# A kernel of two transformer blocks: the output projection's PSUM banks in another order, and VectorE's last gated rows ahead of a feed

## What is computed

```python
mod = jax.nn.silu(c) @ w_ada + b_ada
sh1, sc1, gt1, sh2, sc2, gt2 = jnp.split(mod, 6, axis=-1)
h = adaln(rms_norm(x, g_mix), sh1, sc1)
proj = h @ w_in
...
y_a = swa_attention(q_a, k_a, v_a, sinks) @ w_o_swa
y_b = moba_attention(q_b, k_b, v_b) @ w_o_moba
mixed = jax.nn.sigmoid(gate_a) * y_a + jax.nn.sigmoid(gate_b) * y_b
x = x + gt1[:, None, :] * (mixed @ w_out)
h = adaln(rms_norm(x, g_mlp), sh2, sc2)
u = jnp.square(jax.nn.relu(h @ w_up))
x = x + gt2[:, None, :] * (u @ w_down)
```

## Time and profile before

| | us |
|---|---|
| median of three runs | 1648.8 |
| the three runs | 1648.47, 1648.8, 1655.24 |
| span of the profiled execution | 1650.3 |
| TensorE matmuls busy | 1508.9 (91%) |
| TensorE weight loads busy | 1280.3 (78%) |
| VectorE busy | 1239.3 (75%) |
| ScalarE busy | 867.1 (53%) |
| GpSimd busy | 226.0 (14%) |

### The profile page before, as it was taken

The page is one execution under the profiler, slowest core; times in us unless marked ns, Lnnn a source line. Parts: engine busy times, 40 slices in busy tenths (PEclk is TensorE's granted clock), DMA queues, the critical chain, the costliest instruction groups (busy, mean ns, idle before and its releaser), DMA issues.

```text
span 1650.3 us, 24315 instructions
## 1 busy us (share of the span) xinstructions
PE 1508.9 (91%) x9872; PEld 1280.3 (78%) x9872; DVE 1239.3 (75%) x1845; ACT 867.1 (53%) x1194; POOL 226.0 (14%) x203
## 2 busy tenths in 40 slices
PE   2999989999999998999999899999879779799986
PEld 2889888999998977899998477767568547577764
DVE  4868898888877865899986578877468783688862
ACT  2537536445444642544545467766434474477752
POOL 5050010000005000000002310034111202210121
PEclk7899999999999999999999999999969999999998
DMA  9854497999964448588880499999657421799973
GB/s 321 279 171 138 153 327 269 324 316 319 307 200 135 148 141 297 183 283 294 282 293 26 179 357 422 423 375 400 250 193 252 157 102 54 268 402 422 420 281 140
DMA packets 191871, 425.00 MB, mean 258 GB/s; under 512 B 8344, under 2 KB 136784, under 8 KB 175504
## 3 DMA queue, kind: packets, MB, share of 16 engines
q1 hardware_dynamic: 170688, 334.53, 56.8%
q0 software_dynamic: 13824, 63.62, 10.3%
q10 hardware_dynamic: 7248, 25.30, 3.8%
HBM read 397.20 MB, written 26.21 MB: 257 GB/s over the span
## 4 chain that ended last, share of the span: by engine, by line
PE 66%; DVE 15%; DMA 9%; ACT 6%; issue 3%; POOL 1%; SPq 0%; POOLq 0%; ACTq 0%; DVEq 0%
PE psum L700 62%; DVE acc L1956 4%; DVE w_lo L1933 3%; DMA h_row<-h_rows,token_at 3%; PE psum L1163 2%; DMA raw<-in_w_ada 1%; DMA dn_raw<-in_moe_wd 1%; DVE gu_lo L1968 1%; ACT att_room L1866 1%; ACT w_hi L1431 1%; DVE steps_room L2028 1%; DVE tmp L1989 1%; DMA both<-y_rows,row_at 1%; ACT gu_hi L1445 1%; DVE x L2440 1%
## 5 line engine op out<-in xcount | busy, mean ns | idle before, releaser
L1933 DVE TENSOR_TENSOR w_lo<-raw,w_hi 128x1024 fp32r<-128x1024 f32 x250 | 304.5, 1260 | 75.7 <-ACT w_hi L1431 75.5
L700 PE MATMUL psum<-h_lo,w_hi 128*128 128x256 f32 (+1 forms) x1280 | 341.3, 290 | 0.0
L700 PE MATMUL psum<-h_hi,w_lo 128*128 128x256 f32 (+1 forms) x1280 | 341.1, 289 | 0.2 <-DVE w_lo L1933 0.2
L1431 ACT ACTIVATE w_hi<-raw 128x2048 fp32r<-128x2048 f32 x125 | 238.7, 1911 | 101.4 <-DMA raw<-in_w_up 50.4
L700 PE MATMUL psum<-h_hi,w_hi 128*128 128x256 f32 (+1 forms) x1280 | 264.2, 299 | 9.3 <-DVE tmp L2170 5.7
L1956 DVE SCALAR_TENSOR_TENSOR acc<-raw,cond,acc 128x1024 f32<-128x1024 f32 x196 | 258.3, 1325 | 11.4 <-DMA raw<-in_w_ada 6.8
L700 PEld LDWEIGHTS psum<-h_lo,w_hi 128*128 128x128 f32 x1280 | 250.8, 196 | 1.5
L700 PEld LDWEIGHTS psum<-h_hi,w_lo 128*128 128x128 f32 x1280 | 250.5, 196 | 1.8 <-DVE w_lo L1933 0.5
L700 PEld LDWEIGHTS psum<-h_hi,w_hi 128*128 128x128 f32 x1280 | 200.0, 197 | 32.1 <-issue 17.4
L1968 DVE TENSOR_TENSOR gu_lo<-raw,gu_hi 128x1024 fp32r<-128x1024 f32 x160 | 188.5, 1221 | 28.1 <-ACT gu_hi L1445 28.1
L1445 ACT ACTIVATE gu_hi<-raw 128x2048 fp32r<-128x2048 f32 x84 | 159.9, 1905 | 0.0
(11 more groups left out here) (264 smaller groups left out, 2687.5 us busy)
## 6 DMA issues: line engine op xcount, KB each, us to landing
raw<-in_w_ada SPq DMA_DIRECT2D x48, 1024.0 KB, 6.9
raw<-in_w_mod SPq DMA_DIRECT2D x48, 1024.0 KB, 5.7
raw<-in_w_in SPq DMA_DIRECT2D x34, 1024.0 KB, 5.4
raw<-in_w_up SPq DMA_DIRECT2D x32, 1024.0 KB, 6.0
raw<-in_w_down SPq DMA_DIRECT2D x32, 1024.0 KB, 5.9
raw<-in_moe_wg SPq DMA_DIRECT2D x32, 1024.0 KB, 11.3
raw<-in_moe_wu SPq DMA_DIRECT2D x32, 1024.0 KB, 10.3
dn_raw<-in_moe_wd SPq DMA_DIRECT2D x32, 1024.0 KB, 9.8
```

The lines of the kernel that those rows point to most:

```text
L700: return e.matmul(o, lhs, rhs, start=start, stop=stop, skip_group_check=True)
L1431: e.activation(flat_unit(w_hi[:, split_slot(u)]), raw[:, slot, :], ACT.Copy).then_inc(*w_rounded.on(u))
L1933: e.tensor_tensor(flat_unit(w_lo[:, split_slot(u), k]), raw[:, slot, part], plain(flat_unit(w_hi[:, split_slot(u), k])), ALU.subtract).the ...
```

## The change

1. The output units write banks 2, 3, 0, 1 in place of 0, 1, 2, 3; TensorE and VectorE both follow.
2. On VectorE the low parts of rows 0 and 1 stay where they were. feed(g0+20), which stood at j = 3 behind the sum of row 2, is taken out of there, and so is the low part of row 2. At j = 4, behind the outputs and sum of row 3, now stand the low parts of rows 2 and 3, then feed(g0+20) with its weight unit ahead of its modulation piece, then feed(g0+21).

ScalarE, SyncE and GpSimd keep their orders.

```diff
--- before.py
+++ after.py
@@ -536,6 +536,7 @@
             return head_rstd[:, first + tile // 2 * 2, at_:at_ + 3:2]
 
         GATE_BANKS = (0, 7)
+        OUT_BANKS = (2, 3, 0, 1)
         POOL_BANKS = (0, 1, 2, 3), (4, 6, 7, 0)
 
         paired = {table.batches.index([(row, item[2]) for _, row in conditions(item[1], item[2])]): p
@@ -1016,7 +1017,7 @@
                     close(g)
                 stage = ("m", l)
                 for j in range(4):
-                    b = j
+                    b = OUT_BANKS[j]
                     product(g0 + 21 + j, b, S, h_hi1, h_lo1, lambda i: e.wait_ge(*rounded.at("mix", l, i // 2)),
                             lambda i: e.wait_ge(*rest.at("mix", l, i // 2)))
                     freed[b] = [(added, ("out", l, 2 * j + 1))]
@@ -2160,6 +2161,13 @@
                             normalise(l, h)
                     if k >= 3:
                         pair_lo(l, k - 3)
+                def mix_low(q):
+                    ya = tbuf(2 * (q % 2)).rearrange("p (m n) -> p m n", n=S)
+                    c = slice(2 * q, 2 * q + 2)
+                    e.wait_ge(*rounded.at("mix", l, q))
+                    e.scalar_tensor_tensor(out=h_lo1[:, c, :], in0=ya, scalar=0.5, in1=plain(h_hi1[:, c, :]),
+                                           op0=ALU.mult, op1=ALU.subtract).then_inc(*rest.on("mix", l, q))
+
                 for j in range(9):
                     if 1 <= j <= 4:
                         q = j - 1
@@ -2177,15 +2185,17 @@
                         q = j - 5
                         e.wait_ge(*multiplied.at(g0 + 21 + q))
                         for m in range(2):
-                            add_x(psum[:, q, m * S:(m + 1) * S], l, 2, 2 * q + m, 0).then_inc(
+                            add_x(psum[:, OUT_BANKS[q], m * S:(m + 1) * S], l, 2, 2 * q + m, 0).then_inc(
                                 *added.on("out", l, 2 * q + m))
-                    if j < 8:
+                    if j == 4:
+                        mix_low(2)
+                        mix_low(3)
+                        late = table.feeds[g0 + 20]
+                        feed(g0 + 20, [f for f in late if f[1][0] == "w"] + [f for f in late if f[1][0] != "w"])
+                    if j < 8 and j != 3:
                         feed(g0 + 17 + j)
-                    if 1 <= j <= 4:
-                        e.wait_ge(*rounded.at("mix", l, q))
-                        c = slice(2 * q, 2 * q + 2)
-                        e.scalar_tensor_tensor(out=h_lo1[:, c, :], in0=ya, scalar=0.5, in1=plain(h_hi1[:, c, :]),
-                                               op0=ALU.mult, op1=ALU.subtract).then_inc(*rest.on("mix", l, q))
+                    if 1 <= j <= 2:
+                        mix_low(q)
                 columns(g0 + 24)
                 norm_scale(("m", l))
                 modulate(("m", l))
```

## The result

| kernel | median, us | runs | ratio to before, 95% interval |
|---|---|---|---|
| before | 1650.68 | 20 | 1 |
| the change | 1654.58 | 20 | 1.0024 [1.0013, 1.0035] |
| before, beside the repeat | 1649.85 | 35 | 1 |
| the change, repeated | 1657.47 | 12 | 1.0036 [1.0020, 1.0051] |

The change costs 3.9 us (2.1 to 5.8). Repeated with the last experiments it cost 5.9 us (3.3 to 8.4), and both together, weighted by their intervals, give 1.0028, 4.6 us (3 to 6). It is slower, by less than the 0.5% that the prediction called no change.

A forecast was written before the change was run, and what follows sets the result against it. It took VectorE to bound layer 0 and late columns to hold TensorE in layer 1. 6.05 + 0.35 = 6.4 us on the profiled 1650.3 gave 1656.7, less 1.5 for the median: 1655.2 us, 8-in-10 range 1648.5 to 1659.5.

The forecast's parts named there:

- Layer 1, the columns: Layer 1, ahead of unit 78: columns start 3.55 us later, TensorE's wait grows from 1.96 to 5.5 us.
- Layer 1, the clock: Layer 1, modulation product and unit 78: lowered clock behind the longer wait costs 2.5 us, ends 0 and 3.1.
- What is behind it goes along: Layer 1, behind unit 78: addition, modulation and load all slip with its end, 6.05 us later.
- Rival C: Layer 1: the clock doesn't fall, so +3.55 + 0.35, 1652.7 us; chance 12%.
- Layer 0: +0.35 us: Layer 0: TensorE's won time is given back behind unit 21, net +0.35 us, ends -1.7 and +2.
- the new wait ahead of the squares' sum: Layer 0, behind unit 22: TensorE waits 3.2 us for VectorE's addition.
- Rival A: Layer 0: TensorE's wait sets the stage, -7.7 us there, layer 1 still loses 6.05: 1647 us; chance 7%.
- Rival B: Layer 0: three bunched loads bring unit 24 later than about 235, +2 us; 1657.4 or over; chance 20%.
- Rival D: Both layers: the change reaches layer 1 only in form and does nothing in layer 0; 1655.5 us; chance 3%.
- the lower case of A: Both layers: layer 0's wait is won and layer 1's columns are not held up either; 1641 us; chance 3%.

The follow-up runs named there:

- layer 0 alone: The change with its new VectorE order in layer 0 only, new banks in both layers, against the kernel before: 1649.64 us, 1.0002.
- banks alone: The new bank order with VectorE's order as before, against the kernel before: 1650.58 us, 1.0000.
- piece early: New banks; layer 0's moved modulation piece stays ahead of outputs 3, layer 1 in old order; against the kernel before: 1649.30 us, 0.9991; again 1649.74 us, 0.9989.
- layer 1 alone: The change with its new VectorE order in layer 1 only, new banks in both layers, against the kernel before: 1655.04 us, 1.0030.
- order alone: VectorE's new order in both layers with the old banks 0 to 3, against the kernel before: 1653.29 us, 1.0018.
- five idle matmuls: The change plus five unused matmuls in TensorE's layer 1 wait for the columns; against the kernel before: 1653.32 us, 1.0026; again 1652.19 us, 1.0010.
- ten idle matmuls: The change plus ten unused matmuls of 512 columns ahead of layer 1's modulation product; against the kernel before: 1660.81 us, 1.0069.
- columns still earlier: The piece early kernel with layer 1's columns also moved ahead of the sum of row 3: 1649.74 us, 1.0000 against the kernel before.
- columns-first kernel: The change with the columns of batch 8 written directly behind the sum of row 3, ahead of the low parts: 1650.54 us, 1.0003 against the kernel before.

## Why the prediction was right, and where not

Distances in layer 1 in us, one profile each. "Norm" is the norm's reciprocal; at full clock x56 takes 7.00 and x60 7.45. The first five rows have the old order, the next four the new one. Unit 77's end is the start of the matmuls that follow it (629.24 before), x56 are the matmuls behind the wait for the columns, x60 those behind the load.

| kernel | unit 77 to modulation product | x56 | x60 | both | unit 77 to the norm |
|---|---|---|---|---|---|
| before | 2.91 | 7.00 | 10.47 | 17.47 | 42.92 |
| layer 0 alone | 2.90 | 7.00 | 8.96 | 15.96 | 41.06 |
| banks alone | 2.91 | 8.56 | 8.96 | 17.52 | 42.96 |
| piece early | 2.90 | 8.52 | 8.94 | 17.46 | 42.80 |
| piece early, again | 2.91 | 7.00 | 10.47 | 17.47 | 43.02 |
| **change** | 6.47 | 9.17 | 8.94 | 18.11 | 47.14 |
| change, again | 6.48 | 8.70 | 8.94 | 17.64 | 46.54 |
| layer 1 alone | 6.48 | 8.57 | 8.95 | 17.52 | 46.35 |
| order alone | 6.48 | 9.30 | 7.46 | 16.76 | 45.59 |
| five idle matmuls | 6.48 | 7.00 | 7.45 | 14.45 | 43.49 |
| five, again | 6.48 | 7.00 | 10.47 | 17.47 | 46.56 |
| ten idle matmuls | 9.57 | 6.98 | 10.46 | 17.44 | 49.45 |
| columns still earlier | 2.18 | 8.51 | 7.45 | 15.96 | 40.49 |

**Layer 1, the columns: +3.55 us. Right.** 3.57 us in four profiles, the wait 5.53 for 5.5. That they bound the stage is shown by the columns-first kernel, which takes them back alone and loses the loss.

**Layer 1, the clock: +2.5 us. This step failed.** Behind the wait itself the clock did fall each time: 9.17, 8.70, 8.57 and 9.30 us, 1.6 to 2.3 over full clock, on average 8.94 where the five profiles with the old order have 7.62. But the prediction compared x56 with a kernel before that happened to be at full clock there, and left x60 at its 10.47, the slow value: "What is behind it goes along". In fact the low clock falls behind the first wait, the second, or both, and costs 1.5 to 3.7 us over the two in these nine profiles. Together the two stretches take 17.2 us on average in the old order and 17.5 in the new one: 0.3 us, not 2.5. From the scatter of the nine, that difference is known to about 1 us, so 2.5 is excluded and 1 is not. With 3.57 that is 3.9 us, and the norm comes 3.85 us later on average (46.41 for 42.55), where 6.05 was forecast. The load behind unit 78, put at 5.37 us as the shortest seen, took 5.04 to 5.47 us, which is a few tenths at most. Rival C, at 12%, had the right size of the loss (+3.9, 1652.7) for the wrong reason: the clock does fall, but it fell before too. The Trainium skill, TensorE: Matmul & The Clock Gate, Part 1, says of a kernel's start that the number of slow matmuls differs between runs of the same kernel, and advises against fitting to one count. The traces here show the like in the middle of a kernel (x56 at 7.00 and 8.52 us in two runs of one kernel, behind the same wait of 1.96), which speaks against pricing a slow stretch by one row, as the prediction did.

**Layer 0: +0.35 us, ends -1.7 and +2. Right in its steps but one, a little low in its size.** On the scale of before, the first addition came at 227.2 ("about 227"), the second at 237.5 (237.3), ScalarE started on unit 24 at 233.2 (233.2), the last of three loads was 10.9 us behind the first issue (10.9), and the new wait ahead of the squares' sum was 3.79 us (3.2). The norm came 0.88 us later, and 1.2 us on average over the eight profiles with the new order (41.60 to 42.84 us, average 42.06); the first matmul of the feed-forward part came 1.40 us later, just outside the 1 us that was named. What the prediction missed is one more late load, on the chain of waits of the change in layer 0:

```profile
229.43 8.59 DMA raw<-in_w_up
238.02 0.02 issue
238.04 1.93 ACT w_hi L1432
```

This is the first unit of the feed-forward part. On the scale of before it was issued at 230.9, 1.1 us earlier than there (232.06), and landed 1.4 us after ScalarE took it before (238.0 + 1.5 for 238.16). The bunching reached one load further than unit 24.

**Rival A** (TensorE's wait sets layer 0, 1647 us) is refuted by the kernel with layer 0 alone: the wait is gone and the time is 1.0002. **Rival B**'s point was not reached, 233.2 for 235. **Rival D** holds in its first half, which was in the forecast: in layer 1 there was no gated row to win. Its price doesn't follow from the terms: with nothing in layer 0 the sum is 1648.8 + 6.05 = 1654.9, not 1655.5. Nor does the lower case of A, 1641.1, lie below the 1640.6 that it is counted under. Neither touches the forecast.

**The total.** 6.4 us were forecast on the profiled execution and 1655.2 us in all; 3.9 us and 1654.58 us were measured, 4.6 us with the repeat. By the profiles the sum is 3.9 (layer 1) and 0.9 to 1.2 (layer 0), about 5, with less in layer 0 if part of it is absorbed, which the intervals don't settle. That the forecast of 1655.2 came so near is in part luck: the loss was priced 2.5 us too high (1.8 with the repeat), and the kernel before measured 1.9 us above the median of three runs that the forecast started from.

Still open: whether the idle matmuls help the change (1.8 us, ±2.3), and whether the piece-early kernel is truly faster than the one before (0.9990, ending at 1.0000).

## What to carry to other kernels

Ahead of moving work on an in-order engine, list everything that stands behind the place where it goes in, small instructions too: four of under 0.2 us each, with a waiting TensorE behind them, made this loss, and one line puts them ahead again. If the engine that delivers late is itself full, as VectorE here, its order only chooses where the waiting engine waits (6.97 us in that stage became 6.57); take first the step that empties a slot the loads wait for. And price a lowered clock over a whole stage and several profiles, since it moves from one wait to the next.

## What was not expected of the hardware

- The low clock behind a wait varies in one kernel. In the two profiles of the piece-early kernel the same 56 matmuls took 8.52 and 7.00 us behind the same wait of 1.96 us, and the 60 took 8.94 and 10.47 behind waits of 2.87 and 3.06. With 35 runs of one kernel from 1644.80 to 1657.99 us, 12 runs a kernel can't settle differences of 1 us, though the trace shows distances that differ by less.
- A wait filled with matmuls that nothing uses, down to 1.13 us, was followed by full clock in both profiles (7.00 and 7.00 us), but in one of them the low clock came back at the next wait (10.47 us). The shortness of the wait alone doesn't explain it: an unfilled one of 1.23 us was followed by slow matmuls (8.51 us).
- A load queue that ran dry for 2.3 us (0 GB/s) and then got three loads in 2.7 us needed 10.9 us for the three, and the first load of the feed-forward part, issued 1.1 us earlier than before, still landed at least 1.4 us later.
